# Weight loads split and moved, and a new block order, in a hybrid encoder block on eight cores

## The reference

```python
mod = silu(c) @ w_ada[l] + b_ada[l]
h = _rmsnorm(x, norm1_w[l]) * (1.0 + scale1) + shift1
z = h @ w_in[l] + b_in[l]
q, k, v, u, g_a, g_b = jnp.split(z, split_pts, axis=-1)
...
y_na = _neighbourhood_attention(q, k, v, rpb[l]) @ w_na_out[l]
y_fn = _fourier_mix(u) @ w_fn_out[l] + b_fn_out[l]
merged = jax.nn.sigmoid(g_a) * y_na + jax.nn.sigmoid(g_b) * y_fn
x = x + gate1 * (merged @ w_o[l])
h2 = _rmsnorm(x, norm2_w[l]) * (1.0 + scale2) + shift2
x = x + gate2 * (jnp.square(jax.nn.relu(h2 @ w_mlp_in[l])) @ w_mlp_out[l])
```

## Time and profile before

| what | value |
|---|---|
| median of 3 runs (lowest, highest) | 1591.43 us (1591.37, 1591.84) |
| the profiled execution | 1593.84 us |
| its span, slowest core (core 5) | 1592.3 us |
| spans of the other cores | 1575.8 to 1589.1 us |
| PE, DVE, ACT, POOL busy | 1304.1, 561.1, 448.0, 180.4 us |
| moved by DMA, on one core | 126.08 MB |

### The profile page before, as it was taken

How to read it: one execution, slowest core, us unless ns; L and a number is a source line. 1 busy time by engine, 2 the same in 40 slices (tenths; PEclk the granted TensorE clock), 3 DMA queues, 4 the chain that set the end, 5 groups by cost and what they waited for, 6 DMA issues and landing times.

```text
span 1592.3 us, 20355 instructions; the slowest of 8 cores (1575.8 to 1592.3 us)
## 1 busy us (share of the span) xinstructions
PE 1304.1 (82%) x6772; PEld 611.7 (38%) x6772; DVE 561.1 (35%) x765; ACT 448.0 (28%) x713; POOL 180.4 (11%) x149
## 2 busy tenths in 40 slices
PE   2038768772878869999996999878799999999997
PEld 0013323332555534344342444334344444444443
DVE  0136666651555550000001222248433333333332
ACT  0047457435554540000001222146211211112110
POOL 1000000000000000000000434214150310400000
PEclk8559879885666669999997999988899999999999
DMA  9432222107333116743342100155341312400012
GB/s 150 81 106 68 66 80 61 59 4 123 55 54 54 28 53 172 199 147 135 122 153 54 40 27 14 37 123 212 67 119 27 80 54 33 100 1 1 33 74 106
DMA packets 43157, 126.08 MB, mean 79 GB/s; under 512 B 4656, under 2 KB 17200, under 8 KB 38960
## 3 DMA queue, kind: packets, MB, share of 16 engines
q1 hardware_dynamic: 21024, 89.26, 16.6%
q0 software_dynamic: 22032, 35.53, 14.7%
HBM read 151.91 MB, written 8.39 MB: 101 GB/s over the span
## 4 chain that ended last, share of the span: by engine, by line
PE 69%; DMA 11%; DVE 8%; ACT 6%; issue 5%; POOL 1%; DVEq 0%; ACTq 0%; POOLq 0%; SPq 0%
PE ps_all L892 15%; PE ps_all L913 14%; PE ps_all L725 7%; PE ps_all L727 7%; PE ps_all L429 5%; DMA arena<-w_in 4%; PE ps_all L766 4%; PE ps_all L769 4%; PE ps_all L574 3%; DMA arena<-w 2%; PE ps_all L593 2%; PE ps_all L857 2%; PE ps_all L772 2%; PE ps_all L776 2%; DVE arena L359 2%
## 5 line engine op out<-in xcount | busy, mean ns | idle before, releaser
L892 PE MATMUL ps_all<-arena 128*128 128x512 bf16 x1024 | 237.0, 381 | 6.0 <-DVE arena L359 3.4
L913 PE MATMUL ps_all<-arena 128*128 128x512 bf16 x1024 | 223.5, 379 | 0.0
L725 PE MATMUL ps_all<-arena 128*128 128x512 bf16 x512 | 197.8, 386 | 11.8 <-DVE arena L737 9.8
L727 PE MATMUL ps_all<-arena 128*128 128x512 bf16 x512 | 197.8, 386 | 0.0
L896 ACT ACTIVATE arena<-ps_all 128x512 f32<-128x512 f32 x128 | 76.4, 597 | 359.6 <-PE ps_all L892 358.3
L429 PE MATMUL ps_all<-arena 128*128 128x512 bf16 (+1 forms) x544 | 140.2, 418 | 37.4 <-DVE arena L359 37.4
L892 PEld LDWEIGHTS ps_all<-arena 128*128 128x128 bf16 x1024 | 93.9, 98 | 146.5 <-issue 49.5
L913 PEld LDWEIGHTS ps_all<-arena 128*128 128x128 bf16 x1024 | 100.2, 98 | 120.8
L898 DVE SCALAR_TENSOR_TENSOR arena<-ps_all,arena 128x512 bf16<-128x512 f32 x128 | 88.5, 691 | 155.1 <-ACT arena L896 155.1
L919 DVE TENSOR_TENSOR arena<-ps_all,arena 128x1024 f32<-128x1024 f32 x64 | 78.4, 1224 | 137.8 <-PE ps_all L913 137.8
L580 ACT ACTIVATE arena<-ps_all 128x640 bf16<-128x640 f32 x128 | 89.1, 704 | 74.4 <-PE ps_all L574 48.9
(11 more groups left out here) (88 smaller groups left out, 1260.8 us busy)
## 6 DMA issues: line engine op xcount, KB each, us to landing
arena<-dft SPq DMA_DIRECT2D x32, 1024.0 KB, 4.9
arena<-x SPq DMA_DIRECT2D x48, 512.0 KB, 3.7
arena<-w SPq DMA_DIRECT2D x32, 512.0 KB, 3.7
arena<-w_ada POOLq DMA_DIRECT2D x12, 1024.0 KB, 8.4
arena<-w_in POOLq DMA_DIRECT2D x16, 512.0 KB, 6.2
arena<-w POOLq DMA_DIRECT2D x32, 256.0 KB, 4.2
out<-arena SPq DMA_DIRECT2D x16, 512.0 KB, 2.7
arena<-w_o SPq DMA_DIRECT2D x8, 512.0 KB, 3.6
```

Of the source, the lines that this page charges most:

```text
L725: e.matmul(bank(4 + gq), lhsT=Vt[:, g, gq * 256:gq * 256 + 128], rhs=dtab[db][:, 0, ti, :], start=(g == 0), stop=False)
L727: ins = e.matmul(bank(4 + gq), lhsT=Vt[:, g, gq * 256 + 128:gq * 256 + 256], rhs=dtab[db][:, 1, ti, :], start=False, stop=(g == 31))
L892: ins = e.matmul(bank(kf), lhsT=W1q[b][:, kc, fc * 128:(fc + 1) * 128], rhs=h2T[:, kc, tb * 512:(tb + 1) * 512], start=(kc == 0), stop=(kc ...
L913: ins = e.matmul(Dp[:, half * 512:(half + 1) * 512], lhsT=aTq[ab][:, fc, tl * 128:(tl + 1) * 128], rhs=W2q[b][:, fc, half * 512:(half + 1) ...
```

## The change

Six edits. (1) The 8 loads of w_in become 16: eight of the u columns alone into a Tile of their own (t_Wu), then eight of the q, k and v columns (t_W); u projections wait for t_Wu. (2) The block order becomes 5, 0, 6, 1, 7, 2, 4, 3. (3) The bias table is loaded and put through Exp in 3 parts, by kind, instead of 8, by head. (4) w_fn is loaded by "pool" in the DFT stage's last sweep, after its fifth block of matmuls, into the place that Wfn has in the next stage. (5) The load of w_fn at the head of the gate stage goes. (6) The eight w2 pieces of the output projection come after g = 0 to 7 rather than after odd g.

```diff
+        t_Wu = Tile("Wu")
...
         for kc in range(8):
-            dma("pool", Wqkvu[:, kc, :], win_v[:, kc, 0:2048], writes=[t_W])
+            dma("pool", Wqkvu[:, kc, 1536:2048], win_v[:, kc, 1536:2048], writes=[t_Wu])
+        for kc in range(8):
+            dma("pool", Wqkvu[:, kc, 0:1536], win_v[:, kc, 0:1536], writes=[t_W])
...
-        def proj_fm(col0, hts, t_h, n=512):
+        def proj_fm(col0, hts, t_h, n=512, t_w=None):
+            t_w = t_w or t_W
...
-            S.op("pe", mm, reads=[t_W, t_h], writes=[t_bank[k]])
+            S.op("pe", mm, reads=[t_w, t_h], writes=[t_bank[k]])
...
-                        k = proj_fm(1536 + idx * 128, hts, t_h)
+                        k = proj_fm(1536 + idx * 128, hts, t_h, t_w=t_Wu)
...
-        order = [0, 5, 1, 6, 2, 7, 3, 4]
+        order = [5, 0, 6, 1, 7, 2, 4, 3]
...
-        t_btab = [Tile() for _ in range(8)]
-        for i in range(8):
-            dma("pool", btab_v[:, i * 1920:(i + 1) * 1920], btab_d[:, i * 1920:(i + 1) * 1920], writes=[t_btab[i]])
-            S.op("act", lambda e, i=i: e.activation(out=btab_v[:, i * 1920:(i + 1) * 1920],
-                                                    in_=btab_v[:, i * 1920:(i + 1) * 1920], func=AF.Exp),
-                 reads=[t_btab[i]], writes=[t_btab[i]])
+        t_btab = [Tile() for _ in range(3)]
+        btab_d4 = btab_d.rearrange("p (a b c) -> p a b c", a=8, b=3)
+        for kd in range(3):
+            dma("pool", btab[:, :, kd, :], btab_d4[:, :, kd, :], writes=[t_btab[kd]])
+            S.op("act", lambda e, kd=kd: e.activation(out=btab[:, :, kd, :], in_=btab[:, :, kd, :], func=AF.Exp),
+                 reads=[t_btab[kd]], writes=[t_btab[kd]])
...
-                 reads=[t_tmpS[sbi], t_btab[h]], writes=[t_Pb[sbi]])
+                 reads=[t_tmpS[sbi], t_btab[kind]], writes=[t_Pb[sbi]])
...
+        Wfn_pre = V(46 * KB, [128, 4, 1024], BF16)
...
-                S.op("pe", mm, reads=[t_dtab[db]] + t_Vt[sl * 4:sl * 4 + 4], writes=t_acc)
+                pos_op = S.op("pe", mm, reads=[t_dtab[db]] + t_Vt[sl * 4:sl * 4 + 4], writes=t_acc)
+                if sb == 3 and sl == 4:
+                    dma("pool", Wfn_pre, wfn_d.rearrange("(a p) n -> p a n", p=128), writes=[t_Wfn],
+                        extra_deps=[pos_op])
...
-        dma("pool", Wfn, wfn_d.rearrange("(a p) n -> p a n", p=128), writes=[t_Wfn])
...
-            if g % 2 == 1:
-                load_w2_piece(0, g // 2)
+            if g < 8:
+                load_w2_piece(0, g)
```

## The result

The changed kernel takes 1618.96 us (median of 10 runs) against 1591.63 (10 runs of the kernel before, beside it): a ratio of 1.0177, 95% interval 1.0153 to 1.0200, so 1.8% slower. The forecast was 1620. Ratios here, and in the experiments, leave out the runs in which half of the chip ran at a lower clock; where a median isn't quoted, such runs were among the few that there are.

What follows compares the result with a forecast made beforehand. PE carries most, 1304 of 1592 us, so edits count where PE waits. Edits 1, 2, 3, 4 with 5, and 6 sum as 28 + 0 + 3 - 10.5 + 8 = +28.5 on 1591.4: 1620 us, range 1605 to 1635.

Steps and rivals of the forecast that it cites:

- the line through two rows: w_in loads: 5.59 us for 1 MB and 4.54 for half give 3.49 without bytes; eight added loads cost 27.9 us.
- each writes the Tile of the one before it: Prologue: all sixteen w_in loads run one at a time, a u and q, k, v pair taking 9.1 us.
- a first x load near 113: End of the prologue: with sixteen w_in loads the first x load comes near 113 us instead of 85.12.
- if near 103, the fixed part was over-read: Prologue: a first x load near 103 us would mean a load's cost apart from its bytes was taken too large.
- The rival with block 4 at 37: Projections: block 4 preparing block 3 runs like a full block, likely 37 us, +12, total 1632 us; chance 0.13.
- I leave the last landing at 382.7: Bias table: same bytes, so the last part still lands at 382.7 us; only the wider Exp adds 2.8 us.
- The slow start stays: Head of the gates: PE's first 8 matmuls still take 3.57 us, at the 1.2 GHz level, with w_fn early.
- two or so: Output projection: fewer x loads beside the w1 loads take some two us off the 11.7 of three more groups.
- cheap small loads: Prologue: a u load costs little beyond its bytes, so edit 1 adds 18 us, total 1610 us; chance 0.17.
- serial loads bound by bytes: Prologue and output projection: sixteen w_in loads take the time of eight, w1 loads gain; sum -6.5, 1584 us; chance 0.05.

Runs made afterwards that it cites:

- edit 3 alone: The kernel before with only the bias table loaded and put through Exp in three parts by kind: ratio 1.0039 (1.0023 to 1.0054), +6.2 us.

## Why the prediction was right

The sum of +28.5 us met a measured +27 to +28; the terms did not all meet theirs. In the order of the prediction, by the means over the cores:

- **Edit 1: 28 predicted, 20.0 measured** (20.5 alone). The mechanism, one load at a time behind the barrier, is shown by its removal. The size was off, within its bounds of 18 to 36. The term that was mis-sized is the line through two rows, drawn on to a quarter load. By the means over the cores three quarters cost what the line said (5.1), and a half what its row said (4.6 for 4.54), but a quarter took 3.5, not 4.0: 3 us over the six steps between u loads. About 2 more come from "each writes the Tile of the one before it", which isn't so for the first q, k, v load: it and the last u load passed together in 7.2 us, not 9.1. The first load of all became 2.7 us shorter where the line gave 1.6, and the slow second and third loads of the kernel before (6.4 and 6.0 as means, 1.3 over the usual), which I let stand, don't come back. Together that is 7.3 of the 8 us. The forecast's own witness, a first x load near 113, came at 103.2; "if near 103, the fixed part was over-read" was the case for the quarter. The Trainium skill's formula (DMA: Bandwidth & Descriptors, Anatomy of one DMA) gives 2.6 us for a quarter and 4.4 for a whole megabyte (estimates from that page); from issue to landing a quarter took 2.7 to 3.0 in the chain, a whole 5.03. Its 16 us for the edit missed the measured 20 by 4, from below, and my 28 by 8, from above.
- **Edit 2: 0 predicted, +0.1 in the changed kernel, +1.5 alone** for the stage. Block 4 took 27.1 for 25.5, block 3 36.3 for 35.5. The rival with block 4 at 37 is out. The 2 us in the channel DFT are in no term of the prediction and are told above.
- **Edit 3: +3 predicted, +4.4 measured** (+6.3 alone). The Exp's part was right, 2.7 of 2.8. "I leave the last landing at 382.7" was wrong: the last Exp starts 1.7 us later behind the table's issue in the changed kernel and 3.6 later with edit 3 alone.
- **Edits 4 and 5: -10.5 predicted, -11.1 at the gates' head**, with +1.8 in the position DFT inside that stretch's scatter; alone -9.7 (-13.4 to -6.1). "The slow start stays" was wrong, to the good: the first eight matmuls of the stage took 3.6 us on every core before, and 1.89 to 3.54, 3.0 as a mean, after.
- **Edit 6: +8 predicted, +8.2 measured** (+8.9 alone). Three more groups behind the stop, as worked out; the seven steps of w1 loads took 38.0 us instead of 41.8, where I had put down two or so for that.

So small misses of one sign, +1.4 for the table, +1 in attention, +2.5 in the channel DFT and +1.8 in the position DFT (these last within or near the scatter), stood against -8 for edit 1: part of the closeness of 1620 is luck, and the range, 1605 to 1635, is the fairer statement. The rival "cheap small loads" was nearer than the forecast for its own term and further off for the whole. The rival on the other side, serial loads bound by bytes (1585 us by its own sum, not 1584), is out: sixteen loads cost 20 us more than eight for the same bytes, and the same sixteen in flight together cost 16 less than the eight.

## What to carry to other kernels

Before a load is split so that its first part can be used sooner, look for what else waits for the whole of it: a barrier that collects all DMAs, or a queue that has the work on every part ahead of the first use, leaves only the cost of the pieces. In a scheduler like this one, loads that write one tracked tile run one at a time; give each piece a tile of its own ahead of any splitting or reordering, for in their stages that gained 16 to 18 and 17 us here, where splitting the w_in loads lost 20 and moving the w2 pieces lost 8. And a load that is merely moved early into a stretch with a free queue and a free place keeps its whole gain.

## What the runs showed that I had not expected

- A load's time isn't a line in its bytes down to a quarter: 3.5, 4.6, 5.1 and 5.7 us for 0.25, 0.5, 0.75 and 1 MB read, each with its gap, as means over the cores.
- The bias table's 7.9 MB landed 2 to 4 us later in three strided parts than in eight plain ones, at nearly the same streaming rate (312 against 320 GB/s).
- PE's clock in a stretch of short groups (the channel DFT) has more than one outcome for the same instructions, 34 or 37 us on a core, with a granted clock of 0.82 to 0.87 or of 0.65 to 0.69, and the share of cores with the longer one went with a change two stages earlier.
